# Starting the final gate product on the first turned slices, and halving its last block of columns

## The reference

```
for each layer i:
    mix = attention and convolution branches, gated, @ W_out
    x   = LayerNorm(alpha * x + mix)
    h   = alpha * x + MoE(x)               # 32 experts of 1024, top 4 of them for each token
    x   = LayerNorm(h + sigmoid(h @ w_ple_gate) * (p @ w_ple_proj))
```

## Time and profile before

| | us |
|---|---|
| median of three runs | 1175.01 |
| profiled execution, first to last instruction (its span) | 1173.0 |
| TensorE busy in it | 1134.9 (97%) |
| VectorE busy | 299.7 (26%) |
| ScalarE busy | 173.6 (15%) |
| gate product (line 1253), in the chain that ended last | 27.64 |
| first gate matmul starts | 1137.43 |
| last vector instruction starts | 1169.84 |

### The profile page before, as it was taken

How to read it: one execution, slowest core, us unless ns; L and a number is a source line. 1 busy time by engine, 2 the same in 40 slices (tenths; PEclk the granted TensorE clock), 3 DMA queues, 4 the chain that set the end, 5 groups by cost and what they waited for, 6 DMA issues and landing times.

```text
span 1173.0 us, 13754 instructions
## 1 busy us (share of the span) xinstructions
PE 1134.9 (97%) x5620; PEld 573.9 (49%) x5620; DVE 299.7 (26%) x775; ACT 173.6 (15%) x336; POOL 11.4 (1%) x26
## 2 busy tenths in 40 slices
PE   9999999999999999999889999999999989999997
PEld 7888888734344343434234343443434333334346
DVE  0639842521113111111110211121111111111126
ACT  1213230211111111101010111111111010111112
POOL 0110000000000000000000000000000000000000
PEclk9999999999999999999999999999999999999999
DMA  9996367599999999999999999999999999999970
GB/s 319 353 325 233 109 276 297 217 405 377 430 430 430 431 428 431 429 430 430 429 426 428 430 423 433 429 432 426 434 430 430 430 429 429 423 428 427 425 329 37
DMA packets 60328, 448.16 MB, mean 382 GB/s; under 512 B 6656, under 2 KB 35616, under 8 KB 40544
## 3 DMA queue, kind: packets, MB, share of 16 engines
q1 hardware_dynamic: 52704, 439.79, 90.4%
q10 hardware_dynamic: 7552, 7.38, 1.9%
HBM read 444.53 MB, written 2.62 MB: 381 GB/s over the span
## 4 chain that ended last, share of the span: by engine, by line
PE 78%; DMA 18%; DVE 2%; ACT 1%; issue 1%; SPq 0%; ACTq 0%; DVEq 0%
PE bank L441 45%; DMA arena<-in_w_gu 17%; PE bank L711 10%; PE bank L460 5%; PE bank L418 4%; PE bank L858 2%; PE bank L871 2%; PE bank L1253 2%; PE bank L447 2%; ACT arena L1435 1%; PE bank L784 1%; DMA arena<-in_w_in 1%; PE bank L435 1%; PE bank L1126 1%; PE bank L1186 0%
## 5 line engine op out<-in xcount | busy, mean ns | idle before, releaser
L441 PE MATMUL bank<-arena 128*64 128x512 f32 x3168 | 695.3, 595 | 18.7 <-DMA arena<-in_w_gu 16.3
L441 PEld LDWEIGHTS bank<-arena 128*64 128x64 f32 x3168 | 233.8, 137 | 443.2 <-issue 407.0
L480 DVE TENSOR_TENSOR arena<-bank,arena 128x512 f32<-128x512 f32 x33 | 22.8, 692 | 685.7 <-PE bank L447 685.6
L711 PE MATMUL bank<-arena 128*128 128x256 f32 (+1 forms) x544 | 117.8, 377 | 0.5 <-DMA arena<-in_w_in 0.5
L711 PEld LDWEIGHTS bank<-arena 128*128 128x128 f32 x544 | 101.9, 190 | 15.0 <-DMA arena<-in_w_in 1.1
L1435 ACT ACTIVATE arena<-bank 128x512 f32<-128x512 f32 x62 | 37.0, 597 | 402.8 <-PE bank L441 402.8
L460 PE MATMUL bank<-arena 64*128 64x512 f32 x272 | 67.8, 616 | 0.7 <-ACT arena L1438 0.7
L418 PEld LDWEIGHTS bank<-sel,arena 128*128 128x128 f32 x480 | 54.7, 192 | 11.4 <-issue 11.4
L418 PE MATMUL bank<-sel,arena 128*128 128x128 f32 x480 | 57.6, 278 | 0.0
L1438 ACT ACTIVATE arena<-bank 128x512 f32<-128x512 f32 x32 | 19.1, 597 | 210.3 <-PE bank L441 210.3
L1636 DVE SCALAR_TENSOR_TENSOR arena<-arena 128x256 f32<-128x256 f32 x120 | 48.5, 479 | 0.5 <-DVE arena L1636 0.2
(11 more groups left out here) (213 smaller groups left out, 477.4 us busy)
## 6 DMA issues: line engine op xcount, KB each, us to landing
arena<-in_w_gu SPq DMA_DIRECT2D x45, 4096.0 KB, 31.2
arena<-in_w_dn SPq DMA_DIRECT2D x60, 2048.0 KB, 33.3
arena<-in_w_gu SPq DMA_DIRECT2D x33, 2048.0 KB, 38.7
arena<-in_w_in SPq DMA_DIRECT2D x19, 1024.0 KB, 12.8
arena<-in_w_gu SPq DMA_DIRECT2D x9, 1024.0 KB, 9.1
arena<-in_w_dn SPq DMA_DIRECT2D x6, 1024.0 KB, 9.9
arena<-in_w_out SPq DMA_DIRECT2D x4, 1024.0 KB, 5.1
arena<-in_w_pg SPq DMA_DIRECT2D x2, 2048.0 KB, 32.4
```

What stands on the lines that cost most here:

```text
L441: mm = pe.matmul(to[half * CAP:(half + 1) * CAP, :], rows, w[:, half * 512:(half + 1) * 512], start=first, stop=last)
L711: mm = pe.matmul(bank[n % 4][:, lo:S], w[:, k, j * P:(j + 1) * P], xT_sb[:, k, lo:S], start=(k == 0), stop=(k == KD - 1))
```

## The change

- h is made, turned and copied in five pieces (`H_PARTS`: tile, first slice, number of slices): two of two slices, then three of four. The transposes of piece i go to bank 4 + i % 4.
- TensorE's order is written out: the pieces 0 and 1 are turned, then the first two blocks of tile 0 are begun with the slices 0 and 1, when the first piece's copy is out; the pieces 2, 3 and 4 are turned between parts of these blocks. Tile 0's other blocks and tile 1 follow.
- Tile 1 has five blocks (`PG_PARTS`): three of 256 columns and two of 128. The fifth is in bank 3, and TensorE waits for the fourth sigmoid before it.
- `bn_stats` in tile 1 is over 128 columns at a time, eight in all (two for each block of 256), at `stats2[1]`; tile 0 keeps four over 256.
- VectorE waits for all five pieces of h before it adds h to the first block, where it waited for the piece that it read.

```diff
--- before.py
+++ after.py
@@ -200,6 +200,7 @@
         place = view(o + 1719, LIST)[0:MORE, :]
         iota_c = view(o + 1735, WIDE)
         stats4 = view(o + 1895, 48).rearrange("p (t a b) -> p t a b", t=NT, a=4)
+        stats2 = (stats4[:, 0], view(SC, 48).rearrange("p (a b) -> p a b", a=8))
         assert o + 1943 + 512 <= 31575 + NS * SLOT
         relb_sb = sb("relb_sb", [NB, H])
         wr_sb = sb("wr_sb", [P, KD, NE])
@@ -396,8 +397,12 @@
             return a.rearrange("p (m r) -> p r m", r=r)
 
 
-        def pg_view(k, j):
-            return slot_of(NG + k // 4)[:, (k % 4) * D + j * 256:(k % 4) * D + (j + 1) * 256]
+        H_PARTS = ((0, 0, 2), (0, 2, 2), (0, 4, 4), (1, 0, 4), (1, 4, 4))
+        PG_PARTS = (((0, 256), (256, 256), (512, 256), (768, 256)),
+                    ((0, 256), (256, 256), (512, 256), (768, 128), (896, 128)))
+
+        def pg_view(k):
+            return slot_of(NG + k // 4)[:, (k % 4) * D:(k % 4 + 1) * D]
 
         def mix_bank(t, j):
 
@@ -408,8 +413,8 @@
         def turn_bank(t, j):
             return bank[((0, 1, 4, 5), (4, 5, 4, 5))[t][j]]
 
-        def gate_bank(t, j):
-            return bank[4 * t + j][:, 0:256]
+        def gate_bank(t, part):
+            return bank[(4 * t + part, 3)[part == 4]]
 
         def gather(pe, b=4, ks=range(KD)):
 
@@ -1236,24 +1241,42 @@
                 nc.switch_bb("pe_last", parent=top)
 
 
-                for t in range(NT):
-                    for n in range(2):
-                        pe.wait_ge(h_ready, 2 * t + n + 1)
-                        for k in range(4 * n, 4 * n + 4):
-                            mm = pe.transpose(bank[4 + 2 * t + n][:, (k % 4) * P:(k % 4 + 1) * P],
-                                              h_sb[:, t, k * P:(k + 1) * P], ident)
-                        mm.then_inc(hT_done, 1)
-                for t in range(NT):
-                    pe.wait_ge(hT_out, 2 * t + 2)
-
-                    for j, ks in ((0, range(4)), (1, range(4)), (0, range(4, KD)), (1, range(4, KD)), (2, range(KD)), (3, range(KD))):
-                        for k in ks:
-                            if t == 0 and j == 0 and k % 4 == 0:
-                                pair(NG + k // 4)
-                            mm = pe.matmul(gate_bank(t, j), hT[:, k, t * P:(t + 1) * P], pg_view(k, j),
-                                           start=(k == 0), stop=(k == KD - 1))
-                        if k == KD - 1:
-                            mm.then_inc(pg_done, 1)
+                def turn_h(i):
+                    t, k0, n = H_PARTS[i]
+                    pe.wait_ge(h_ready, i + 1)
+                    for k in range(k0, k0 + n):
+                        mm = pe.transpose(bank[4 + i % 4][:, (k - k0) * P:(k - k0 + 1) * P],
+                                          h_sb[:, t, k * P:(k + 1) * P], ident)
+                    mm.then_inc(hT_done, 1)
+
+                def ple_gate(t, part, ks, turned):
+                    c0, n = PG_PARTS[t][part]
+                    pe.wait_ge(hT_out, turned)
+                    for k in ks:
+                        mm = pe.matmul(gate_bank(t, part)[:, 0:n], hT[:, k, t * P:(t + 1) * P],
+                                       pg_view(k)[:, c0:c0 + n], start=(k == 0), stop=(k == KD - 1))
+                    if k == KD - 1:
+                        mm.then_inc(pg_done, 1)
+
+                turn_h(0)
+                turn_h(1)
+                pair(NG)
+                ple_gate(0, 0, range(2), 1)
+                turn_h(2)
+                ple_gate(0, 1, range(2), 1)
+                ple_gate(0, 0, range(2, 4), 2)
+                ple_gate(0, 1, range(2, 4), 2)
+                turn_h(3)
+                pair(NG + 1)
+                ple_gate(0, 0, range(4, KD), 3)
+                ple_gate(0, 1, range(4, KD), 3)
+                turn_h(4)
+                ple_gate(0, 2, range(KD), 3)
+                ple_gate(0, 3, range(KD), 3)
+                for part in range(4):
+                    ple_gate(1, part, range(KD), 5)
+                pe.wait_ge(pge_ready, 4)
+                ple_gate(1, 4, range(KD), 5)
 
                 pe.br("pe_end")
                 for e in range(NE):
@@ -1526,14 +1549,15 @@
                 a.br_ne(flag, 0, "act_more", "act_last")
                 nc.switch_bb("act_last", parent=top)
 
-                for n in range(2 * NT):
-                    a.wait_ge(hT_done, n + 1)
-                    a.activation(hT[:, 4 * (n % 2):4 * (n % 2) + 4, (n // 2) * P:(n // 2 + 1) * P],
-                                 bank[4 + n][:, :].rearrange("p (k t) -> p k t", k=4), ACT.Identity).then_inc(hT_out, 1)
+                for i, (t, k0, n) in enumerate(H_PARTS):
+                    a.wait_ge(hT_done, i + 1)
+                    a.activation(hT[:, k0:k0 + n, t * P:(t + 1) * P],
+                                 bank[4 + i % 4][:, 0:n * P].rearrange("p (k t) -> p k t", k=n),
+                                 ACT.Identity).then_inc(hT_out, 1)
                 for t in range(NT):
-                    for j in range(4):
-                        a.wait_ge(pg_done, 4 * t + j + 1)
-                        a.activation(pge[:, t, j * 256:(j + 1) * 256], gate_bank(t, j), ACT.Sigmoid).then_inc(pge_ready, 1)
+                    for part, (c0, n) in enumerate(PG_PARTS[t]):
+                        a.wait_ge(pg_done, 4 * t + part + 1)
+                        a.activation(pge[:, t, c0:c0 + n], gate_bank(t, part)[:, 0:n], ACT.Sigmoid).then_inc(pge_ready, 1)
                     a.wait_ge(var2, t + 1)
                     a.activation(rstd[:, t:t + 1], mv[:, t, 1:2], ACT.Sqrt, bias=epsc).then_inc(std2, 1)
 
@@ -1887,32 +1911,36 @@
                 v.br_ne(flag, 0, "dve_more", "dve_last")
                 nc.switch_bb("dve_last", parent=top)
 
-                for n in range(2 * NT):
-                    t, at = n // 2, slice((n % 2) * 512, (n % 2 + 1) * 512)
-                    v.wait_ge(comb_done, n + 1)
-                    nc.vector.scalar_tensor_tensor(h_sb[:, t, at].rearrange("p (r m) -> p r m", r=4),
-                                                   x1[:, t, at].rearrange("p (r m) -> p r m", r=4), ALPHA,
-                                                   in_rows(total[t][n % 2][:, :], 4),
+                for t, k0, n in H_PARTS:
+                    half, r0 = k0 // 4, k0 % 4
+                    at = slice(k0 * P, (k0 + n) * P)
+                    v.wait_ge(comb_done, 2 * t + half + 1)
+                    nc.vector.scalar_tensor_tensor(h_sb[:, t, at].rearrange("p (r m) -> p r m", r=n),
+                                                   x1[:, t, at].rearrange("p (r m) -> p r m", r=n), ALPHA,
+                                                   in_rows(total[t][half][:, :], 4)[:, r0:r0 + n, :],
                                                    ALU.mult, ALU.add).then_inc(h_ready, 1)
 
                 c = Tally()
                 for t in range(NT):
-                    for j in range(4):
-                        at = slice(j * 256, (j + 1) * 256)
-                        v.wait_ge(pge_ready, 4 * t + j + 1)
-                        v.wait_ge(pple_out, 2 * t + j // 2 + 1)
+                    for part, (c0, n) in enumerate(PG_PARTS[t]):
+                        at = slice(c0, c0 + n)
+                        half, m0 = c0 // 512, c0 % 512 // 4
+                        v.wait_ge(pge_ready, 4 * t + part + 1)
+                        v.wait_ge(pple_out, 2 * t + half + 1)
                         nc.vector.tensor_tensor(pge[:, t, at], pge[:, t, at], pple[:, t, at], ALU.mult).then_inc(t_chain, 1)
                         v.wait_ge(t_chain, c.up())
-                        v.wait_ge(h_ready, 2 * t + j // 2 + 1)
+                        v.wait_ge(h_ready, len(H_PARTS))
                         nc.vector.tensor_tensor(pge[:, t, at].rearrange("p (m r) -> p m r", r=4),
                                                 pge[:, t, at].rearrange("p (m r) -> p m r", r=4),
-                                                by_rows(h_sb[:, t, j // 2 * 512:(j // 2 + 1) * 512], 4)[:, j % 2 * 64:(j % 2 + 1) * 64, :],
+                                                by_rows(h_sb[:, t, half * 512:(half + 1) * 512], 4)[:, m0:m0 + n // 4, :],
                                                 ALU.add).then_inc(t_chain, 1)
                         v.wait_ge(t_chain, c.up())
-                        nc.vector.bn_stats(stats4[:, t, j, :], pge[:, t, at]).then_inc(t_chain, 1)
-                        c.up()
+                        wide_part = 256 >> t
+                        for at in range(c0, c0 + n, wide_part):
+                            nc.vector.bn_stats(stats2[t][:, at // wide_part, :], pge[:, t, at:at + wide_part]).then_inc(t_chain, 1)
+                            c.up()
                     v.wait_ge(t_chain, c.n)
-                    nc.vector.bn_aggr(mv[:, t, :], stats4[:, t, :, :]).then_inc(var2, 1)
+                    nc.vector.bn_aggr(mv[:, t, :], stats2[t][:, :, :]).then_inc(var2, 1)
```

## The result

The changed kernel took 1180.56 us (median of four runs, 1176.35 to 1181.98) against 1175.00 for the kernel before in the same rounds (1174.98 to 1175.03): a ratio of 1.0041 with a 95% interval of 1.0028 to 1.0053 (here and below the ratio is an estimate from the single runs and not the quotient of the two medians, which is 1.0047 here). The forecast was 1174.6 us and no measurable change. The kernel is slower by a small amount that is clear of the noise. The run that was profiled is the fastest of the four, 1176.35 us with a span of 1174.6; the other three had spans of 1178.6 to 1180.2 and a lower mean clock (0.988 to 0.993 instead of 0.997). The mean clock alone proves little: the kernel before also had executions with a mean of 0.991 or 0.992 that took about 1175.3 us.

What follows compares the result with a forecast made beforehand. The end was taken as bound by the gate product (27.64 us), its start and the work behind its last matmul. Terms -1.25 + 1.31 + 0.12 - 0.59 = -0.41 gave 1174.6 us, range 1173.8 to 1175.2.

Steps and rivals of the forecast that it cites:

- The head: Start of the gate product: first matmul 1.25 us earlier, 12 transposes woven in later cost 1.31; sum +0.06 us.
- The last block: Tile 1's end: 16 records of 256 columns become 32 of 128, last gate value 0.12 us later.
- the rival of 1177.0 us: Last block: weight loads without overlap pace the 128-column matmuls, +2.54 us instead of +0.12; chance 3%.
- The tail: Work behind the last matmul, on 128 columns instead of 256: -0.59 us, aggregation over 48 values included at +0.03.
- The square root: Rival behind the last sigmoid: root's table load delays the reciprocal, 1174.7 us (10%), or 1175.5 if over 0.58 us (1%).
- The end in sum: Head, last block and tail together: -1.25 + 1.31 + 0.12 - 0.59 = -0.41 us.
- 1175.01 - 0.41: Whole kernel: the end's sum taken off the median of the runs, what lies around the span untouched: 1174.6 us.
- small drifts in the long stretch that DMA paces: Stretch paced by DMA: drifts there were taken in by the range of 1173.8 to 1175.2 us.
- the mean clock of 0.997: TensorE's clock, whole kernel: read as granted in full throughout, the 2.4 GHz level.
- the change would stay within 0.2%: Whole kernel: 95% for a change within 0.2% (2.35 us), 3% for faster, 2% for slower; forecast 0.03%.

Runs made afterwards that it cites:

- the head alone: Kernel before with only h in five pieces and TensorE's woven order, tile 1's last block whole: 1175.36 us; with 99 unreached instructions added, 1175.31 us.
- the tail alone: Kernel before with only tile 1's last block in two of 128 columns and bn_stats of 128 columns there: 1175.66 us, ratio 1.0010.
- 222 take it away: Changed kernel with 222 unreached TensorE instructions behind its end, two-round blocks 256 instructions further back than in the kernel before: 1174.99 us, ratio 0.9998.
- shift of 34: Two-round blocks 34 TensorE instructions further back than before: changed kernel 1180.56 and, repeated, 1179.89 us; kernel before with 34 unreached instructions 1181.65 us.
- (60): Kernel before with 60 unreached TensorE instructions ahead of the two-round blocks: 1179.83 us, ratio 1.0036.
- with 32: Kernel before with only tile 1's last block split, which makes the end's code 32 TensorE instructions longer: 1175.66 us, ratio 1.0010.
- with 17: Kernel before with 17 unreached TensorE instructions ahead of the two-round blocks: 1175.37 us, ratio 1.0007.
- the layout put right: Changed kernel with 100 unreached TensorE instructions (134 in all against the kernel before): 1174.98 us; with 222 (256 in all): 1174.99 us.
- a shift of 100: Only the last block's split, plus 68 unreached instructions, two-round blocks 100 instructions further back than in the kernel before: 1174.98 us, ratio 0.9998.

## Why the prediction was wrong

By its own steps:

- *The head* (-1.25 + 1.31 = +0.06 us): measured +0.13 in the head alone. The first gate matmul came 1.27 us earlier (2.92 us behind the combination's start instead of 4.19); the 12 transposes cost 1.39, since the product's last matmul starts 28.80 us behind its first instead of 27.41. Right.
- *The last block* (+0.12 us): the tail alone has its last sigmoid at +32.14 us from the combination's start, 32.02 before. Right. The 32 records of 128 columns start 0.112 us apart, so the weight loads overlap, and the rival of 1177.0 us was wrong.
- *The tail* (-0.59 us): from the last sigmoid's start to the aggregation's end 1.75 us instead of 2.24, so -0.49. The aggregation over 48 values takes 0.37 and not 0.29 us:

```profile
L1256 PE MATMUL bank<-arena 128*128 128x128 f32 x32 | 3.7, 275 | 0.0
...
L1943 DVE BATCH_NORM_AGGREGATE arena<-arena 128x2 f32<-128x48 f32 x1 | 0.4, 373 | 0.0
```

- *The square root*: it starts with the aggregation's end, 0.21 us after its table load has ended (1168.86 to 1169.07), so nothing of the load shows on the path; the rival is out.
- *The end in sum* was -0.41; measured -0.24, of the right sign.
- *The step that failed* is the last one, "1175.01 - 0.41". It set everything ahead of the combination equal, but for "small drifts in the long stretch that DMA paces". I counted each added instruction where it runs and none where it lies. TensorE's end stands ahead of the blocks of two rounds in its program, and one of these blocks is executed on this data; the trace of before showed its two waits marked "issue", 2.43 and 0.48 us, and the instruction queue's four packets around them. What the runs showed in place of zero: 2.1 us of stall instead of 0.5, which left the two short executions of the changed kernel at 1175.52 and 1176.35 us, and 2 to 6 us more in the eight long ones of ten; in the one of these that was profiled, and in its like with 34 unreached instructions, the clock had fallen behind the stall.
- *A smaller slip*: the first paragraph reads the mean clock of 0.997 as full clock throughout. The trace of before has 3.4 us at half clock at 940.8 us (and 5.7 us behind the last matmul). It changes nothing in the sum, but it was the sign that TensorE's clock can fall in this loop.

The forecast that the change would stay within 0.2% failed by this step alone; that the end's own sum came out with the right sign is borne out by the rows, and the totals are too coarse to confirm it.

What is shown: that placement alone makes the loss (34 unreached instructions bring it, 222 take it away), where it begins, and that a long stretch at half clock stands behind the second wait (shift of 34, twice) or behind the first and through the second (60) in the three profiles of such executions over 1178 us. What isn't: why the executions of one kernel part, with a shift of 34 mostly long (13 of 15), with 32 two of 11, and with 17 one to three of 11. No run here settles it.

Why TensorE is late by a certain amount at the end also takes more than the stall. In the changed kernel's first profile it is 2.7 us late behind the block. At the waits for the weights at 943.1 and 1001.5 us it is 1.7 late, as late as the weights are, and 1.8 at the combination. In between, short stretches at half clock, which fall at other places in the two executions (940.8 us before, 1002.8 after), take this to 0.3 and to 3.4.

With the layout put right, the change as a whole (1174.98 and 1174.99 us) is 0.2 to 0.3 us under the kernel before, inside what these runs can tell. The tail alone with a shift of 100 has 1174.98 us as well. None of the three is shown to be faster.

## What to carry to other kernels

An added instruction has a place as well as a cost: list what lies behind it in its engine's program and is reached by a branch, and look in the trace for waits marked "issue" behind such branches, since their length depends on where a piece of code ends. Before a small gain or loss is put down to an edit, run the old kernel with as many unreached instructions in that place. Blocks that hardly ever run, laid ahead of ones that do, and the end moved far away, can cost more than the edit gains: each jump of TensorE into code that wasn't there yet cost 1.6 to 3.9 us here, and in some executions its clock.

## What the hardware showed that I had not expected

- Behind a taken branch the packets of TensorE's code started 6.1 us apart in the kernel before (608.7, 614.8, 620.9 us), and 5.6 to 6.2 us lay between the first two in the other profiles with a second wait. So a first piece that held less work left TensorE idle: 0.48, 0.90, 1.86, 2.12 and 5.28 us at shifts of 0, 17, 32, 34 and 60 (2.07 and 2.50 in two other profiles at 34). TensorE went on 2.4 to 2.6 us behind a packet's start each time.
- Two waits of 1.8 to 2.8 us, with 3.6 us of work between them, in a stream that was busy otherwise, stood ahead of 10.2 and 13.7 us at half clock in two of the three profiles with a shift of 34. In the third (1176.35 us), and in the one with 32, the clock held. With the half clock TensorE was up to 10.4 us late at that place.
- The loss is not additive. The loop, in part paced by its weights, gave back 0.9 us of 2.7 in one execution (the changed kernel's first profile, from 620 us on), 2.1 of 10.4 in another (34 unreached instructions) and 3.4 of 8.4 in a third (60).
